# Product 5 of the convolution groups as seven quarter products, beside product 4

## The reference, cut to what matters

```python
h = rmsnorm(x, norm_g[layer])
proj = h @ w_in[layer]                     # 1024 x 1024 times 1024 x 12288
b_a, c_a, x_a, z_a, q, k, v, z_b, g_a, g_b = jnp.split(proj, split_points, axis=-1)
# short convolution branch
u = c_a * x_a
u = causal_depthwise_conv3(u, conv_w) + conv_b
y_a = (b_a * u * silu(z_a)) @ w_a_out
y_b = retention_branch(q, k, v, z_b, w_b_out[layer])
merged = sigmoid(g_a) * y_a + sigmoid(g_b) * y_b
x = x + merged @ w_o[layer]
```

## Time and profile before

| | us |
|---|---|
| median of 3 runs | 1368.4 |
| the profiled execution's span, first to last instruction | 1366.5 |
| TensorE busy | 1354.6 |
| VectorE busy | 1063.1 |
| ScalarE busy | 591.4 |
| GpSimd busy | 473.3 |

### The profile page before, as it was taken

How to read it: one execution, slowest core, us unless ns; L and a number is a source line. 1 busy time by engine, 2 the same in 40 slices (tenths; PEclk the granted TensorE clock), 3 DMA queues, 4 the chain that set the end, 5 groups by cost and what they waited for, 6 DMA issues and landing times.

```text
span 1366.5 us, 16902 instructions
## 1 busy us (share of the span) xinstructions
PE 1354.6 (99%) x6498; PEld 1138.4 (83%) x6498; DVE 1063.1 (78%) x1053; ACT 591.4 (43%) x801; POOL 473.3 (35%) x349
## 2 busy tenths in 40 slices
PE   9999999999999999999999999999999999999997
PEld 7888888888888888888888888888888888888886
DVE  6898474578877777788888888747776998788887
ACT  7843233323222233234333333438778434433445
POOL 0100232244555554555555666415454001100002
PEclk9999999999999999999999999999999999999999
DMA  9746313322212222355443444657767699945443
GB/s 338 215 128 216 114 56 124 124 77 77 77 50 63 74 62 62 109 154 154 138 140 124 116 146 141 198 193 254 264 229 261 142 327 312 233 164 200 161 86 124
DMA packets 106128, 212.74 MB, mean 156 GB/s; under 512 B 6977, under 2 KB 49089, under 8 KB 101185
## 3 DMA queue, kind: packets, MB, share of 16 engines
q1 hardware_dynamic: 103024, 193.82, 42.4%
q0 software_dynamic: 2880, 17.83, 6.6%
q10 hardware_dynamic: 144, 0.02, 0.0%
HBM read 148.20 MB, written 55.05 MB: 149 GB/s over the span
## 4 chain that ended last, share of the span: by engine, by line
PE 95%; issue 1%; ACT 1%; DVE 1%; POOL 1%; DMA 0%; SPq 0%; POOLq 0%; DVEq 0%; ACTq 0%
PE psum L2488 16%; PE psum L2489 16%; PE psum L2486 16%; PE psum L2623 7%; PE psum L2625 7%; PE psum L2624 7%; PE psum L2413 4%; PE psum L2415 4%; PE psum L2416 4%; PE psum L2430 2%; PE psum L2432 2%; PE psum L2431 2%; PE psum L2531 2%; PE psum L2533 2%; PE psum L2532 2%
## 5 line engine op out<-in xcount | busy, mean ns | idle before, releaser
L2488 PE MATMUL psum<-hc,slots 128*128 128x512 f32 x976 | 379.8, 389 | 0.0
L2486 PE MATMUL psum<-hc,slots 128*128 128x512 f32 x976 | 379.8, 389 | 0.0
L2489 PE MATMUL psum<-hc,slots 128*128 128x512 f32 x976 | 379.8, 389 | 0.0
L1088 ACT ACTIVATE slots<-work 128x1024 fp32r<-128x1024 f32 (+1 forms) x158 | 162.0, 1036 | 435.9 <-PE psum L2489 329.0
L1583 DVE TENSOR_TENSOR slots<-work,slots 128x1024 fp32r<-128x1024 f32 (+1 forms) x158 | 228.6, 1448 | 39.0 <-ACT slots L1088 39.0
L2489 PEld LDWEIGHTS psum<-hc,slots 128*128 128x128 f32 x976 | 183.2, 188 | 38.1
L2486 PEld LDWEIGHTS psum<-hc,slots 128*128 128x128 f32 x976 | 183.2, 188 | 37.5
L2488 PEld LDWEIGHTS psum<-hc,slots 128*128 128x128 f32 x976 | 183.2, 188 | 37.3
L1348 ACT ACTIVATE last_slot<-arena 128x1024 fp32r<-128x1024 f32 x112 | 118.6, 1062 | 163.0 <-PE psum L2625 156.8
L2623 PE MATMUL psum<-last_slot 128*128 128x512 f32 (+1 forms) x452 | 175.3, 388 | 0.0
L2625 PE MATMUL psum<-last_slot 128*128 128x512 f32 (+1 forms) x452 | 175.0, 387 | 0.0
(11 more groups left out here) (214 smaller groups left out, 2331.2 us busy)
## 6 DMA issues: line engine op xcount, KB each, us to landing
work<-w_channel SPq DMA_DIRECT2D x80, 512.0 KB, 3.7
arena<-w_last SPq DMA_DIRECT2D x19, 1024.0 KB, 7.5
qk<-qk_scratch SPq DMA_DIRECT2D x32, 512.0 KB, 3.4
arena<-w_last POOLq DMA_DIRECT2D x9, 1024.0 KB, 11.4
v_raw<-value_scratch SPq DMA_DIRECT2D x32, 256.0 KB, 3.7
arena<-gate_scratch SPq DMA_DIRECT2D x16, 512.0 KB, 7.1
value_c<-w_value SPq DMA_DIRECT2D x10, 512.0 KB, 4.8
rows_of_x<-x_rows SPq DMA_DIRECT2D x8, 512.0 KB, 8.8
```

What stands on the lines that cost most here:

```text
L1088: nc.scalar.activation(slots[:, u % SLOTS, 0, 0:columns_of(u)], src, ACT.Copy).then_inc(w_hi, 1)
L2486: nc.tensor.matmul(bank, slot[:, 0, w], x_high, start=product in STARTS and j == 0, stop=False, skip_group_check=True)
L2488: nc.tensor.matmul(bank, slot[:, 0, w], x_low, start=False, stop=False, skip_group_check=True)
L2489: last = nc.tensor.matmul(bank, slot[:, 1, w], x_high, start=False, stop=j == 3, skip_group_check=True)
```

## The change

In the eight convolution groups, product 5 is also taken as seven quarter products, as units 5a (place 3) and 5b (place 8, `FIFTH_HALF`), between product 2 and product 7. For it

- `hx` holds the combinations of product 5 while 5a and 5b run and those of product 4 while 4a and 4b do. Both sets are stored once in DRAM (`hx_d`, 1.5 MB each); SP loads product 5's set once the group before has ended and product 4's set once 5b has (`load_hx`, first T4, then T1 and T2). T3 takes a quarter's place in `hc` here too.
- GpSimd makes four more weight sums a group (`second_sums(g, 5)`), queued behind `conv_gate(g-1, 2)` and ahead of `second_sums(g, 4)`.
- ScalarE and VectorE split 768 columns for 5a and 1024 for 5b where they split 1024 once.
- VectorE adds 5a's quarter (`second_first(g, 5)`, at 5b's place) and the rest (`second_rest(g, 5)`, after 5b) to `tp_first`, then `add(g, 5)`.
- x's quarters for product 5 are summed and subtracted in group 1 (`t5_quarter`, `t_sum`) and split in group 2 (`fifth_high` at place 1, `fifth_low` at place 2).

```diff
+FIFTHS = CONVS
+LAST_HALF, FIFTH_HALF = 7, 8
+UNIT_TABLE = [(g, p) for g in range(GROUPS) for p in (0, 1, 2, 3, FIFTH_HALF, 4, 5, 6, LAST_HALF)
+              if (p != FIFTH_HALF or g in FIFTHS) and (p != LAST_HALF or g in TWICE)]
...
 def columns_of(u):
+    if u < VALUE_UNITS:
+        return 2 * HALF
+    g, n = place_of(u)
+    return 3 * QUARTER if n == 6 and g in TWICE or n == 3 and g in FIFTHS else 2 * HALF
...
+        def load_hx(product):
+            n = int(product == 5)
+            sp.dma_start(hx[:, 2].bitcast(F32), hx_d[n, :, 2]).then_inc(t4_in, 16)
+            sp.dma_start(hx[:, 0:2].bitcast(F32), hx_d[n, :, 0:2]).then_inc(t1_t2_in, 16)
         for g in range(GROUPS):
+            if g == 1:
+                sp.wait_ge(h_ready, made(3) + 3)
+                sp.dma_start(hx_d[0], hx[:, :].bitcast(F32)).then_inc(fifth_kept, 16)
+            if g in FIFTHS and g > FIFTHS.start:
+                sp.wait_ge(unit_done, ended_at(g - 1) + 1)
+                load_hx(5)
...
+            if g == FIFTHS.start:
+                sp.wait_ge(h_ready, made(3) + 8)
+                sp.dma_start(hx_d[1], hx[:, :].bitcast(F32)).then_inc(fifth_kept, 16)
             if g + 1 < GROUPS:
-                sp.wait_ge(w_ready, unit_at(g, 5) + 1)
+                sp.wait_ge(w_ready, fifth_ended_at(g) + 1)
                 load_work(g + 1, "d", 3)
                 sp.wait_ge(w_ready, unit_at(g, 7) + 1)
                 load_work(g + 1, "b", 2)
                 sp.wait_ge(w_ready, unit_at(g, 3) + 1)
                 load_work(g + 1, "c", 1)
+            if g in FIFTHS:
+                sp.wait_ge(unit_done, fifth_ended_at(g) + 1)
+                if g == FIFTHS.start:
+                    sp.wait_ge(fifth_kept, 80)
+                load_hx(4)
             if g:
                 stores[kind_of(g - 1)](g - 1)
...
+            if g in FIFTHS:
+                second_sums(g, 5)
             if g in TWICE:
-                second_sums(g)
+                second_sums(g, 4)
...
-                if n == 7:
-                    act.wait_ge(summed, second_summed(g, 4))
+                if n in (LAST_HALF, FIFTH_HALF):
+                    act.wait_ge(summed, second_summed(g, product, 4))
...
+            if g == FIFTHS.start and p == 1:
+                for name in ("T1", "T2", "T4", "T3"):
+                    fifth_high(name)
...
+        def second_first(g, product):
+
+            dve.wait_ge(unit_done, unit_at(g, product) + 1)
+            at = (tp_v if product == 4 else tp_first)[g % 2][:, 0, 0:QUARTER]
+            nc.vector.tensor_tensor(at, psum[:, second_bank(g, product), 0:QUARTER], at, ALU.add).then_inc(value_sum, 1)
...
+                elif n == 3 and g in FIFTHS:
+                    second_first(g, 5)
+                elif n == FIFTH_HALF:
+                    second_rest(g, 5)
+                    add(g, 5)
                 elif ORDER[n] not in (1, 2):
                     add(g, ORDER[n])
 
-            if u + 2 < UNITS and (u < VALUE_UNITS or place_of(u)[1] < 7):
+            if u + 2 < UNITS and (u < VALUE_UNITS or place_of(u)[1] != LAST_HALF):
                 low(u + 2)
...
+            if g == FIFTHS.start - 1 and p in (1, 2):
+                for n in range(2):
+                    t5_quarter(2 * (p - 1) + n)
+            if g == FIFTHS.start - 1 and p in (4, 5):
+                for name in (("T1", "T3"), ("T2", "T4"))[p - 4]:
+                    t_sum(name, t5_quarters, t5_sums, 20)
+            if g == FIFTHS.start and p == 2:
+                for name in ("T1", "T2", "T4", "T3"):
+                    fifth_low(name)
...
+            loads = hx_loads(g, product) if g in FIFTHS else 0
             pe.wait_ge(w_ready, u + 1)
-            pe.wait_ge(sum_made, 5 * g + sums_until(ORDER, 7))
+            pe.wait_ge(sum_made, 5 * g + sums_until(ORDER, before(ORDER, product)))
...
+            if loads:
+                pe.wait_ge(t4_in, 16 + 16 * loads)
             product_of_quarters(u, 2, second("T4"), c21).then_inc(unit_done, 1)
             pe.wait_ge(w_ready, u + 2)
+            if loads:
+                pe.wait_ge(t1_t2_in, 16 + 16 * loads)
             product_of_quarters(u + 1, 2, second("T1"), five, start=True)
             product_of_quarters(u + 1, 3, second("T3"), seven, start=True)
             product_of_quarters(u + 1, 1, quarter(3), c12)
-            pe.wait_ge(value_sum, second_added(g, 1))
+            pe.wait_ge(value_sum, second_added(g, product, 1))
             product_of_quarters(u + 1, 0, second("T2"), one_six).then_inc(unit_done, 1)
...
-                if product == 4 and g in TWICE:
-                    second_units(g)
+                if product == 4 and g in TWICE or product == 5 and g in FIFTHS:
+                    second_units(g, product)
                 else:
                     unit(g, product)
```

More of the change, by code:

```diff
@@ L108, in ended_at, with fifth_ended_at, product_at @@
     return unit_at(g, 4) + (g in TWICE)
+def fifth_ended_at(g):
+    return unit_at(g, 5) + (g in FIFTHS)
+def product_at(n):
+    return 5 if n == FIFTH_HALF else ORDER[min(n, 6)]
 def columns_of(u):
[L113 removed]
+    if u < VALUE_UNITS:
+        return 2 * HALF
+    g, n = place_of(u)
+    return 3 * QUARTER if n == 6 and g in TWICE or n == 3 and g in FIFTHS else 2 * HALF
 def place_of(u):
@@ L121, in summed_until, with second_summed, second_added, hx_loads @@
 def summed_until(g):
[L123 to L133, removed]
+    return 16 + 4 * g + 4 * len([n for n in TWICE if n < g]) + 4 * len([n for n in FIFTHS if n < g])
+def second_summed(g, product, n):
+    return summed_until(g) + 4 + 4 * (product == 4 and g in FIFTHS) + n
+def second_added(g, product, n):
+    return 20 + 4 * (g - TWICE.start) + 4 * len([f for f in FIFTHS if f < g or f == g and product == 4]) + n
+def hx_loads(g, product):
+    return 2 * (g - FIFTHS.start) + (product == 4)
 def before(order, product):
@@ L450, in made, with x_quarter, second_part, second_bank @@
         return (8 if name == "raw" else 12) + 2 * MADE.index(name) + count
[L452 to L461, removed]
+    def x_quarter(product, n, part):
+        return hc[:, KEPT_AT[product], part, 2 * (n // 2):2 * (n // 2) + 2, n % 2 * QUARTER:(n % 2 + 1) * QUARTER]
+    def second_part(product, name, part):
+        return x_quarter(product, 1, part) if name == "T3" else hx[:, ("T1", "T2", "T4").index(name), part]
+    def second_bank(g, product):
+        return set_at(g + 1, 6 if product == 4 else 1)
     def tiles(first, count=2):
@@ L896, in s4, with second_sums @@
             nc.gpsimd.tensor_tensor(a, c, a, ALU.subtract).then_inc(summed, 1)
[L898 to L902, removed]
+        def second_sums(g, product):
+            w = work[ROLES[g]["d" if product == 4 else "e"]]
+            a11, a12, a22, a21 = (w[:, n * QUARTER:(n + 1) * QUARTER] for n in range(4))
+            pool.wait_ge(w_ready, unit_at(g, product) + 1)
             nc.gpsimd.tensor_tensor(a22, a21, a22, ALU.add).then_inc(summed, 1)
             nc.gpsimd.tensor_tensor(a21, a11, a21, ALU.subtract).then_inc(summed, 1)
-            pool.wait_ge(summed, second_summed(g, 1))
+            pool.wait_ge(summed, second_summed(g, product, 1))
             nc.gpsimd.tensor_tensor(a11, a22, a11, ALU.subtract).then_inc(summed, 1)
-            pool.wait_ge(summed, second_summed(g, 3))
+            pool.wait_ge(summed, second_summed(g, product, 3))
             nc.gpsimd.tensor_tensor(a12, a12, a11, ALU.subtract).then_inc(summed, 1)
@@ L2458, in unit @@
             if product == 4 and g == TWICE.stop:
-                pe.wait_ge(x_in[4], 80)
+                pe.wait_ge(kept_in, 80)
+            if product == 5 and g == FIFTHS.stop:
+                pe.wait_ge(fifth_kept, 112)
             if product == 6 and g - 1 in TWICE:
-                pe.wait_ge(value_sum, second_added(g - 1, 4))
+                pe.wait_ge(value_sum, second_added(g - 1, 4, 4))
             if g == 0:
```

104 lines of the change are left out of this document (65 added, 39 removed).

## The result

The changed kernel takes 1404.65 us (median of 5 runs, 1403.97 to 1405.99) against 1368.4 before, a ratio of 1.0266 (95% interval 1.0253 to 1.0278). The forecast was 1408, range 1384 to 1416. The profiled span is 1404.2 us against 1366.5, 37.7 more.

A forecast was written before the change was run, and what follows sets the result against it. TensorE, busy throughout a 37.60 us group, was taken as the bound. Stalls of 3.0 and 2.4 us in seven groups (37.5), with small terms for g = 2 and 1, made 39.5: 1368.4 + 39.5 = 1408 us, range 1384 to 1416.

The forecast's parts named there:

- TensorE's gain: In 8 convolution groups product 5 takes 4.95 us instead of 5.44, 0.49 a group, 3.9 us in all.
- The lock and its turns: VectorE operations reading two SBUF tensors, taps included, take turns with GpSimd operations; additions out of PSUM never lengthen.
- the higher of the two sums: Group's head with tap 1 waiting for GpSimd's sums: 3.0 us lost; the other, with free taps, 1.8.
- The head: Group start to product 7, g = 3 to 9: new sums delay 5b's split and second_first(g, 5), 3.0 us lost a group.
- E: Start of product 7, counted from the start of the group's product 1; forecast at 24.75 us instead of 21.76.
- The tail: Product 7 to next group: turns with s1 and s3 delay conv_product and second_first(g, 4), 2.4 us lost a group.
- The sum: Groups 3 to 9 lose 7 x (3.0 + 2.4) = 37.5 us, g = 2 1.6, g = 1 some 0.4; 39.5 in all.
- All engines then stand to the next group as now: At the end of the tail: engines stand to the next group as before the change, so the stalls repeat each group.
- rival (a): Only one of the two stalls occurs: about 1389 us with the head's alone, 1386 with the tail's; chance 0.2.
- The loads (d): x's combinations: forecast at no cost, covered by the stall; rival: late T1 adds 1 to 2 us a group, chance 0.09.
- Rival (c): Added work is hidden, second_first(5) and second_first(4) come in time, and 3.9 us are gained: 1364.5 us; chance 0.06.

The follow-up runs named there:

- run 5: Changed kernel with quarter sums in a buffer of their own, made earlier, second_first(g, 5) ahead of conv_early, group 1's sums one place earlier: 1369.17 us, ratio 1.0004.
- run 6: Changed kernel with only the separate buffer and new places of the quarter sums, second_first(g, 5) staying behind conv_early: 1375.46 us, ratio 1.0050.
- run 8: Kernel of run 5 with second_first(g, 5) also ahead of the low part of product 7 on VectorE: 1369.48 us, ratio 1.0003.
- run 2: Changed kernel without GpSimd's four quarter sums for product 5, the weight quarters split as they are: 1391.51 us, ratio 1.0168.
- run 1: Changed kernel with conv_product(g, 1) moved behind second_first(g, 4) on VectorE: 1406.44 us, ratio 1.0276.
- run 4: Changed kernel with run 1 and run 2 together, conv_product(g, 1) moved and product 5's sums left out: 1383.51 us, ratio 1.0111.
- run 7: Changed kernel with only second_first(g, 5) put ahead of conv_early on VectorE: 1406.05 us, ratio 1.0274.
- run 9: Kernel of run 8 with TensorE waiting for conv_early only before product 7's second 12 matmuls: 1368.01 us, ratio 0.9996.
- run 3: Changed kernel without the loads of x's combinations and TensorE's waits for them, both products using one set: 1405.83 us, ratio 1.0270.
- run 11: Kernel of run 9 with the last of product 5's four quarter sums made after tap 1: 1371.78 us, ratio 1.0025.
- run 12: Kernel of run 11 with the third quarter sum moved after tap 1 as well: 1374.63 us, ratio 1.0047.

## Why the prediction was right, and where its numbers were off

**TensorE's gain, 0.49 a group: right.** Groups without any wait take 37.11 (g = 2 in runs 5, 6 and 8); 37.60 - 37.11 = 0.49. The estimate from the Trainium skill, "TensorE: Matmul & The Clock Gate", section "Back-to-back issue gap", was 0.59; the trace decides.

**The lock and its turns: right.** Every operation with two SBUF inputs that meets GpSimd in these rows is longer, and tap 1 too: 1.64 for 1.28, as the higher of the two sums had it. add(6) out of PSUM kept its 1.21. That agrees with the rule of the Trainium skill, "SBUF — State Buffer", section "Who interferes with whom". Tap 0, which has one tensor input and takes its factors from columns, stood in the turns as well: in each of groups 3 to 9 of the changed kernel it ended 0.55 after gate multiply 2, and sum 1 ended 0.59 after it.

**The head: right in every step, 0.3 too long.** By g = 6, forecast and measured: split of 5a over at 11.0 and 11.02, tap 0 at 12.7 and 12.72, tap 1 at 14.6 and 14.40, sum 4 at 16.8 and 16.51, low 5b at 19.25 and 18.92, conv_y at 21.7 and 21.37, second_first at 23.95 and 23.60, E at 24.75 and 24.47. 2.7 lost instead of 3.0. Run 2 shows the cause: without the sums 0.36 of 2.31 is left. The 0.3 lies in the handing over: an operation that waited for its turn ended less than its full length after the other (tap 1 1.09 after sum 1, where 1.28 was added; sum 1 0.59 after tap 0, not 0.74).

**The tail: right in every step, 0.35 too long.** Counted from E, s1 over at 13.0 and 12.82, low of product 1 at 14.1 and 13.91, s3 at 16.45 and 16.14, conv_product at 17.05 and 16.69, second_first at 17.4 and 17.03, the next group at 18.2 and 17.87. 2.0 lost instead of 2.4. Of this 0.25 is the start: second_rest begins 0.20 after E, not 0.45. The rest is the same handing over, and that rows on one engine overlap by some 0.08, which I had added up as if they didn't.

**The sum: its terms were too large, and one was missing.** Groups 3 to 9 cost 34.5, not 37.5; g = 2 cost 1.54 (1.6 forecast); g = 1 nothing (0.4). Not forecast at all: g = 10 at 1.6, with no wait in it, and about 1.2 of the 34.5, both from the clock (last section). Together 37.7 in the span where 39.5 stood. Without the clock it would have been 34.9: that the forecast came so near is in part luck, because stalls priced 0.65 a group too high stood in for a loss that it didn't have. The other 1.5 of the 3.4 us between forecast and result are not a fault of the sum: the profiled execution took 1405.99 us, 1.8 above its span, close to the forecast's 1.9, and is 1.3 longer than the median one.

**"All engines then stand to the next group as now": true of this kernel, though no reason was given.** It holds because TensorE waits in the tail until VectorE has caught up. Runs 1 and 4, in which it doesn't wait there, show the lateness going on into the next head. For the same reason rival (a), one stall of the two, was not to be had by the exchanges tried: 1, 4 and 7 took a wait away or shortened it and got it back elsewhere, whole or in part (1: 2.0 out of the tail, 1.8 into the head).

**The loads (d): right at nothing, for a wrong reason.** The cover named for them, the stall, isn't needed: in runs 5, 8 and 9 there is hardly a stall, and no wait ended by a DMA. The step that failed is that the loads would land one after the other, 15.4 after E. In g = 6 of the changed kernel product 4's set is issued at 430.25 and 430.72 and lands 4.8 and 7.8 us later, which is 9.0 after E, 4.0 before T1 is wanted. In run 9 the load of T1 and T2 issued at 449.37 in g = 7 lands 8.2 us later, 10.9 after E, still 2 early.

**Rival (c), 1364.5: not reached.** It asked for second_first(5) by 20.6 and second_first(4) by 15.1 after E. Run 9 has the first, at t = 20.0, but the second only at 15.5 after E: TensorE, which has lost 0.2 at products 7 and 3 by then, waits for it, and the time ends where the kernel before was. VectorE is in that group's head without an idle stretch from t = 0.2 to conv_early, so each step further is taken from the next one. Whether another order gives the 3.9 us is open.

## What to carry to other kernels

When engines run ordered lists and hand buffers to one another in a cycle, price a change by how much it lengthens the loop round all engines; in runs 1, 7 and 8 taking the wait away from the engine that showed it, or shortening it, moved it to another place. GpSimd's small sums kept their length beside VectorE's additions out of PSUM (0.73 and 0.74), and a buffer of their own, with the earlier places that it allows, took back 29 of 36 us. Before moving an operation, look up what the one behind it waits for: it may stand in a gap that is free.

## What the runs showed of the hardware

After a stall of about 2 us the clock sometimes falls, though nothing differs in the program. In the changed kernel the wait in g = 5 ends at 386.24; these are the windows behind it and two matmuls:

```profile
387.05:388.50 1.45, 1.45 (x7) 1.12 (x6) 1.42 (x3) 0.85 (x1) 0.00 (x0) 0.60 0.65 243
388.50:391.00 2.50, 2.50 (x8) 1.98 (x7) 2.36 (x4) 0.00 (x0) 0.00 (x0) 0.55 0.92 315
391.00:405.00 14.00, 13.66 (x81) 11.96 (x80) 7.77 (x7) 2.76 (x3) 9.25 (x7) 1.00 0.39 131
```

```profile
388.06 0.63 PE L2589 MATMUL psum<-hc,slots 128*128 128x512 f32 x1
388.49 0.63 PE L2591 MATMUL psum<-hc,slots 128*128 128x512 f32 x1
```

Matmuls of 512 columns stand 0.43 apart instead of 0.227, near the 1.2 GHz level, for some 3.5 us, and TensorE is busy 39.55 us in that group instead of 37.88. Yet the group is only 0.17 longer than g = 6 (42.51 and 42.34): the loop over VectorE and GpSimd sets its length, and the slow stretch eats TensorE's later wait. Of the groups 3, 4, 5 and 8 of the changed kernel, all at a mean clock of 0.96, only g = 4 is 0.9 longer. There the clock is low already when the wait for second_first(g, 5) ends (g = 4 starts at 319.36):

```profile
343.04 0.58 PE L2522 MATMUL psum<-hx,slots 128*128 128x256 f32 x1 [2.30 <-DVE tp_first L1800]
344.49 0.63 PE L2589 MATMUL psum<-hc,slots 128*128 128x512 f32 x1
```

The last six matmuls of product 5 take 1.45 us instead of 0.81, so E is 25.13 instead of 24.47, and VectorE's second_rest(g, 5) with all that follows it round the loop is later by as much. In g = 3 and 5 the clock falls after E, and only product 7 is slow. In run 3 it is the same: g = 4 and 8, with the fall before those six matmuls, take 43.2, g = 3, 5, 7 and 9, with the fall after E, 42.5. In run 2 each of five groups is 0.9 longer, and in g = 10, where no wait is left to eat, it costs 1.6. Which groups are hit differs: with the loads left out they are 3, 4, 5, 7, 8 and 9. What decides it stays open. In the runs whose longest wait in these groups is 1.32 us or less (4, 5, 6, 8, 9, 11 and 12) the clock falls in none of them.
